# Moving weight blocks and activation blocks by lines of 64 bytes in a two-block transformer kernel, with matmuls in groups of two or four chunks

## What is computed

```python
# first stack, per layer
h = layer_norm(ALPHA * h + 0.5 * swiglu(h, ffn1...), ln1_g, ln1_b)
proj = h @ w_in                      # 20 column blocks of 128
mix = concatenate([ssd, fox, mla]) @ w_out
h = layer_norm(ALPHA * h + mix, ln2_g, ln2_b)
h = layer_norm(ALPHA * h + 0.5 * swiglu(h, ffn2...), ln3_g, ln3_b)
# second stack, per layer
x = x + 0.5 * swiglu_2(rmsnorm(x, ...), ffn1...)
x = x + mixers(rmsnorm(x, ...) @ w_in) @ w_out
x = x + 0.5 * swiglu_2(rmsnorm(x, ...), ffn2...)
```

## Time and profile before

| | us |
|---|---|
| median of three runs | 1946.86 (1946.73 to 1949.25) |
| profiled execution, its own time | 1947.75 |
| span of the profiled execution | 1945.9 |
| TensorE matmul busy | 1931.2 (99%) |
| TensorE weight load busy | 1892.7 (97%) |
| VectorE busy | 1431.5 (74%) |
| ScalarE busy | 1019.8 (52%) |
| GpSimd busy | 152.7 (8%) |

### The profile page before, as it was taken

One profiled execution on the slowest core, in us unless ns is written; L12 is line 12 of the kernel. 1 busy time (PEld: TensorE's weight loads), 2 busy tenths in 40 slices (PEclk: granted clock), 3 DMA queues, 4 the chain that ended last, 5 costly groups with the idle time before them and its releaser, 6 DMA issues.

```text
span 1945.9 us, 42335 instructions
## 1 busy us (share of the span) xinstructions
PE 1931.2 (99%) x16150; PEld 1892.7 (97%) x16150; DVE 1431.5 (74%) x2591; ACT 1019.8 (52%) x1527; POOL 152.7 (8%) x192
## 2 busy tenths in 40 slices
PE   9999999999999999999999999999999999999998
PEld 8999989999999999899999999999999999999998
DVE  6774787987588768879978874667765775667763
ACT  4443687554455447865547443665445444565443
POOL 0001123000100011320010100000000000100000
PEclk9999999999999999999999999999999999999999
DMA  7454433545454544345553665445555555435554
GB/s 265 172 197 170 166 109 112 192 174 193 156 192 172 196 164 145 109 152 194 201 191 140 235 233 183 151 149 185 193 214 177 195 202 208 152 131 195 194 213 154
DMA packets 46830, 346.66 MB, mean 178 GB/s; under 512 B 5344, under 2 KB 6416, under 8 KB 9232
## 3 DMA queue, kind: packets, MB, share of 16 engines
q1 hardware_dynamic: 44416, 335.63, 48.0%
q0 software_dynamic: 2320, 9.74, 1.6%
HBM read 344.29 MB, written 1.07 MB: 177 GB/s over the span
## 4 chain that ended last, share of the span: by engine, by line
PE 91%; DVE 4%; ACT 2%; DVEq 1%; issue 1%; DMA 0%; ACTq 0%; SPq 0%; POOL 0%
PE ps L622 22%; PE ps L623 22%; PE ps L624 22%; PE ps L639 14%; PE ps L630 2%; PE ps L631 2%; PE ps L632 2%; DVE w_lo L1996 1%; PE ps L1162 0%; DVE pj L2465 0%; DMA h<-in_hidden 0%; DVE cst L2486 0%; PE ps L1197 0%; DVE pj L2462 0%; ACT scratch L1669 0%
## 5 line engine op out<-in xcount | busy, mean ns | idle before, releaser
L1996 DVE TENSOR_TENSOR w_lo<-raw,w_hi 128x1024 fp32r<-128x1024 f32 (+1 forms) x582 | 749.3, 1313 | 151.1 <-ACT w_hi L1300 91.5
L622 PE MATMUL ps<-x_hi,w_lo 128*128 128x256 f32 (+3 forms) x2208 | 622.1, 282 | 1.5 <-DVE x_lo L2087 0.6
L624 PE MATMUL ps<-x_hi,w_hi 128*128 128x256 f32 (+3 forms) x2208 | 615.1, 279 | 0.0
L623 PE MATMUL ps<-x_lo,w_hi 128*128 128x256 f32 (+3 forms) x2208 | 614.8, 278 | 0.0
L1297 ACT ACTIVATE w_hi<-raw 128x1024 fp32r<-128x1024 f32 x454 | 466.3, 1052 | 92.5 <-PE ps L639 49.0
L622 PE MATMUL ps<-hid_hi,w_lo 128*128 128x256 f32 (+1 forms) x1536 | 431.5, 281 | 0.1
L624 PE MATMUL ps<-hid_hi,w_hi 128*128 128x256 f32 (+1 forms) x1536 | 430.2, 280 | 0.0
L623 PE MATMUL ps<-hid_lo,w_hi 128*128 128x256 f32 (+1 forms) x1536 | 429.8, 280 | 0.0
L622 PEld LDWEIGHTS ps<-x_hi,w_lo 128*128 128x128 f32 x2208 | 414.9, 188 | 6.4 <-issue 4.2
L623 PEld LDWEIGHTS ps<-x_lo,w_hi 128*128 128x128 f32 x2208 | 415.0, 188 | 0.5
L624 PEld LDWEIGHTS ps<-x_hi,w_hi 128*128 128x128 f32 x2208 | 414.6, 188 | 0.0
(11 more groups left out here) (351 smaller groups left out, 2315.3 us busy)
## 6 DMA issues: line engine op xcount, KB each, us to landing
raw<-in_w_up SPq DMA_DIRECT2D x176, 1024.0 KB, 4.8
raw<-in_w_down SPq DMA_DIRECT2D x64, 1408.0 KB, 6.0
raw<-in_w_in SPq DMA_DIRECT2D x36, 1024.0 KB, 4.8
raw<-in_w_out SPq DMA_DIRECT2D x16, 1024.0 KB, 4.8
cst<-row_copy POOLq DMA_DIRECT2D x2, 1088.0 KB, 8.5
raw<-in_w_up SPq DMA_DIRECT2D x4, 512.0 KB, 7.2
cst<-in_consts POOLq DMA_DIRECT2D x1, 1537.5 KB, 6.5
prm<-in_prm POOLq DMA_DIRECT2D x2, 690.0 KB, 7.2
```

Source lines behind the costliest of these rows:

```text
L622: mm(dst, low, xa, start=first, stop=False)
L623: mm(dst, high, xb, start=False, stop=False)
L624: return mm(dst, high, xa, start=False, stop=last)
L1996: v.tensor_tensor(dst, src, high.bitcast(F32), ALU.subtract).then_inc(lo_done, 1)
```

## The change

It moves operands and reorders matmuls. The arithmetic is the same, and so is the number of matmuls. Core of the diff:

```diff
-        PLAIN_LO = [KD * X_PITCH + n * LINE for n in (0, 0, 5, 6)]
-        PLAIN_AT, PLAIN_W = 640, max(PLAIN_LO) + KD * X_PITCH
+        PLAIN_AT, PLAIN_W = 640, 2 * KD * X_PITCH
...
-        x1_hi, x1_lo = chunks(x_hi_all[:, 2 * LINE:], KD, X_PITCH), chunks(x_lo_all, KD, X_PITCH)
+        x1_hi, x1_lo = chunks(x_hi_all, KD, T1), chunks(x_lo_all, KD, T1)
+        cat1_hi, cat1_lo = chunks(x_hi_all[:, 2 * LINE:], KD, X_PITCH), chunks(x_lo_all, KD, X_PITCH)
...
+        def plain_of(T):
+            pitch = T1 if T == T2 else X_PITCH
+            return chunks(plain, KD, pitch), chunks(plain[:, KD * pitch:], KD, pitch)
+
+        GROUP = {T1: 4, T1 + 2: 2, T2 + 2: 4}
         TIGHT = Place(P, 0, 0)
-        OPENING = Place(P, LINE, LINE)
-        BESIDE_274 = Place(P + 2 * LINE, 3 * LINE, LINE)
+        OPENING = Place(P + LINE, 0, 2 * LINE)
+        BESIDE_274 = Place(P + 2 * LINE, LINE, 3 * LINE)
         LEVEL_274 = Place(P + 2 * LINE, LINE, 3 * LINE)
-        BESIDE_258 = Place(P + 2 * LINE, LINE, 0)
+        BESIDE_258 = Place(P + LINE, 2 * LINE, 0)
+
+        ENTRY = {0: Place(P + 2 * LINE, 3 * LINE, LINE), 1: Place(P + 2 * LINE, 0, 2 * LINE)}
+
+        def entry_place(level):
+            return ENTRY.get(level, TIGHT)
...
-            def three_beside(dst, high, low, xa, xb, first, last):
...
-            def in_pairs(dst, high, low, xa, xb, T):
+            def in_groups(dst, high, low, xa, xb, T, size):
 
-                for k in range(0, KD, 2):
+                for k in range(0, KD, size):
                     for w, x in ((low, xa), (high, xb), (high, xa)):
-                        for c in (k, k + 1):
+                        for c in range(k, k + size):
                             last = mm(dst, w[:, c, :], x[:, c, 0:T], start=w is low and c == 0,
                                       stop=w is high and x is xa and c == KD - 1)
...
-                if T == T1 + 2 and place is not TIGHT:
-                    last = in_pairs(dst, high, low, xa, xb, T)
+                if T in GROUP and place is not TIGHT:
+                    last = in_groups(dst, high, low, xa, xb, T, GROUP[T])
...
-                N = T + 4 if T == T2 else T + 2
-                xs, place = (plain_hi, plain_lo_of(LEVEL_NORM[norm])), level_place(T)
+                N, xs, place = T + 2, plain_of(T), level_place(T)
...
-                unit(turn0, 1, 0, second_pieces)
-                unit(turn0, 1, 1)
+                entry = entry_place(LEVEL_NORM[norm])
+                unit(turn0, 1, 0, second_pieces, entry)
+                unit(turn0, 1, 1, {}, entry)
```

More of the change, by code:

```diff
@@ L304, in cat1 @@
         def cat1(T):
-            return x_of(T)
+            return (xt_hi, xt_lo) if T == T2 else (cat1_hi, cat1_lo)
         def hid_of(T):
@@ L624, in three @@
                 return mm(dst, high, xa, start=False, stop=last)
-            def three_beside(dst, high, low, xa, xb, first, last):
-                if first:
-                    mm(dst, high, xa, start=True, stop=False)
-                mm(dst[:, 0:T2 + 2], low, xa[:, 0:T2 + 2], start=False, stop=False)
-                step = mm(dst[:, 0:T2], high, xb[:, 0:T2], start=False, stop=False)
-                return step if first else mm(dst, high, xa, start=False, stop=last)
-            def in_pairs(dst, high, low, xa, xb, T):
-                for k in range(0, KD, 2):
+            def in_groups(dst, high, low, xa, xb, T, size):
+                for k in range(0, KD, size):
                     for w, x in ((low, xa), (high, xb), (high, xa)):
-                        for c in (k, k + 1):
+                        for c in range(k, k + size):
                             last = mm(dst, w[:, c, :], x[:, c, 0:T], start=w is low and c == 0,
@@ L667, in first_pair @@
                         high, low = (narrow_at(w, TIGHT, 0, u)[:, k, :] for w in (w_hi, w_lo))
-                        step = three_beside if T == T2 + 4 else three
-                        last = step(ps[:, bank + u, 0:T], high, low, xa[:, k, 0:T], xb[:, k, 0:T],
-                                    n == 0, n == KD - 1)
+                        last = three(ps[:, bank + u, 0:T], high, low, xa[:, k, 0:T], xb[:, k, 0:T],
+                                     n == 0, n == KD - 1)
                         if n == KD - 1:
@@ L1315, in hi_next, with second_pair @@
                 hi_unit(j, u, W_NARROW, place)
-            def second_pair(turn, u):
+            def second_pair(turn, u, place=TIGHT):
                 act.wait_ge(raw_landed[1], turn * 16 + 16)
                 act.wait_ge(unit_used, turn * 4 + (u - 1 + START))
-                hi_unit(1, u, W_NARROW)
+                hi_unit(1, u, W_NARROW, place)
             def load_log_exp():
@@ L2135, in level_down @@
                     if last and not crossing:
-                        lo_unit(turn0 + DOWN_T, 1, 0, W_NARROW)
+                        lo_unit(turn0 + DOWN_T, 1, 0, W_NARROW, entry_place(after[0] if after else None))
                     dve.drain()
@@ L2174, in level_up @@
                 ha, hb = hid_of(T)
-                def columns(block, n):
-                    if T == T2:
-                        v.tensor_reduce(wsum[:, 2 * n:2 * n + 2], block[:, T:T + 4].rearrange("p (h c) -> p c h", h=2), AX_X, ALU.add)
-                        dve.drain()
-                        return wsum[:, 2 * n + 1:2 * n + 2]
-                    v.tensor_copy(wcol[:, n:n + 1], block[:, T:T + 1])
-                    return block[:, T + 1:T + 2]
                 def pair(it, j, width):
@@ L2187, in pair @@
                     dve.wait_ge(unit_used, turn0 * 4 + it * 4 + (2 * j + 1 + START))
-                    v.scalar_tensor_tensor(out=silu[:, j, 0:T], in0=neg_mean[:, 0:T], scalar=columns(gate, 2 * j),
+                    v.tensor_copy(wcol[:, 2 * j:2 * j + 1], gate[:, T:T + 1])
+                    v.scalar_tensor_tensor(out=silu[:, j, 0:T], in0=neg_mean[:, 0:T], scalar=gate[:, T + 1:T + 2],
                                            in1=gate[:, 0:T], op0=ALU.mult, op1=ALU.add)
@@ L2196, in pair @@
                     dve.wait_ge(unit_used, turn0 * 4 + it * 4 + (2 * j + 2 + START))
[L2197 removed]
+                    v.tensor_copy(wcol[:, 2 * j + 1:2 * j + 2], upb[:, T:T + 1])
+                    v.scalar_tensor_tensor(out=half, in0=neg_mean[:, 0:T], scalar=upb[:, T + 1:T + 2],
                                            in1=upb[:, 0:T], op0=ALU.mult, op1=ALU.add).then_inc(up_free, 1)
```

37 lines of the change are left out of this document (15 added, 22 removed).

## The result

Seven executions of each kernel, taken in turn: 1953.6 us after (1953.4 to 1953.75), 1949.1 us before (1946.73 to 1949.6), ratio 1.0031 with a 95% interval of 1.0022 to 1.0040. Against the 1946.9 us from which the forecast was made it is 6.7 us more. The profiled execution after took 1953.73 us, its span 1951.9.

What follows compares the result with a forecast made beforehand. TensorE's matmul pace, start to start, was taken to bound the kernel, with no wait or transfer able to give much. Terms -3.6 - 2.0 - 0.3 = -5.9 us took 1946.9 to 1941.0 us, range 1936.0 to 1947.4.

Steps and rivals of the forecast that it cites:

- Opening: Opening loop, 960 matmuls of 272 columns: constant distance takes them from 123.7 to 120.0 ns each, 3.6 us less.
- the signs named in advance: Signs of a wrong forecast, among them opening loop at 123 ns or more, or widely spread durations in constant-distance loops.
- The other bound, 125.1: Opening loop: pace per matmul in ns if it took the uneven state's overhead, 113.3 + 11.8; 1.3 us more.
- 258 columns: Loop of the 256-token level stage, 960 matmuls: from 118.8 to 116.7 ns each, 2.0 us less.
- Level loops: 274-column loops, code inside unchanged: either may end up even or uneven; no net change, bounds 2.6 us either way.
- The two entered alike: The two 274-column level loops: claimed entered alike before the change, yet came out differently, at 123.3 and 126.0 ns.
- Second pairs -0.3, in-projections nothing: Second pairs of the 274-column level stages: 0.3 us less together; in-projections at distance 2 instead of 0: no change.
- The rule weighed against it: TensorE's two read ports are independent and never wait, so no distance in lines matters: sum 0.0 against -5.9 us.
- D: Rival: constant distance locks all these loops into the uneven state, 4.4 us slower, 1951.3 us; chance 0.08.
- C: Rival: distance in lines has no effect, overheads follow from columns and entry; 1946.9 us; chance 0.16.
- A: Rival: everything lands, and the second level loop and the in-projections turn even too; 1937.4 us; chance 0.20.
- B: Rival: one of the two new loops lands, the other stays or turns uneven; about 1944 us; chance 0.18.

Runs made afterwards that it cites:

- the one of 4530 us: One execution of the changed kernel with opening and 256-token level stage taken back, left out, cause unknown: 4530.2 us; the other ten had median 1949.1 us.

## Why the prediction was wrong, point by point

**What bounds the kernel**: right. TensorE's pace decided it all; no wait, queue or transfer took part, before or after.

**Opening, -3.6 forecast, +2.0 measured.** The step that failed is "I take 120.0, by the row that is nearest: 272 is, as 256, a whole number of lines, and both are continuous". None of some 140 stretches of 272 columns, over five combinations of pitches and three orders, came below 123.3 ns. 256 columns do not carry to 272: the good pattern of 256 takes 113.3, that of 272 takes 123.3, 10 ns more for 6.7 ns of columns, and as much as 274 columns in their even state. Nor was continuity what made 256 columns fast: at distance 0 they have it too and take 120.0 ns. The opening before, at 123.7, was within 0.4 ns of the best of all these stretches, so at most 0.4 us was to be won. Of the signs named in advance the loop at 123 or more came; the wide spread of durations did not (285 to 291 ns, before 284 to 291), though the step was wrong. The other bound, 125.1, was too low by 0.7 as well: uneven patterns cost different amounts in different layouts.

**258 columns, -2.0 forecast, +2.9 in the loop, +2.4 in the stage, +2.1 to 2.4 in the time.** The step that failed is "Nearest is the 274-column loop ... even state 107.5 + 9.2 = 116.7". An overhead was carried from one layout to another, and from distance 0 to 3. What the runs put in its place: 121.8 ns at distance 3, and 118.5 at 2, where the overhead is 11.0. At distance 2 the stage gains 0.7 us in the trace and some 0.5 by kind of execution, at distance 3 it loses 2.4.

**Level loops, no net change forecast.** The bounds were right, the middle was not. With the change's second pairs both loops were uneven in all three profiles, and every time but the one of 4530 us fits that; before, one of them was even in 31 of 74 executions. Against the executions from which I started this is the full 2.6 us. Of these the starting point is partly luck: from the upper kind of before, 1949.3, the same change costs 4.3 us. "The two entered alike" was the wrong reading here: their second pairs differ, and the slower kind went with the uneven loop each time.

**Second pairs -0.3, in-projections nothing**: the second pairs gave 0.1, the in-projections nothing, 1949.2 and 1949.1 in the two runs. The 0.3 was too much: from starts rounded to 0.1 us the slower second pair was read at 129 ns, where the trace has 127.8, and in pairs it runs at 126.0 and not at the even 123.3.

**VectorE, weight writes, DMA, nothing**: right.

**The rule weighed against it.** The Trainium skill, SBUF — State Buffer, "Who interferes with whom", gives TensorE independent ports for the two streams and lets it wait for nobody. With every other engine idle, 256 columns took 113.3 ns or 120.0 and 258 columns 118.4 or 121.7, by the addresses alone. The measurement decides: the sum by that rule, 0.0, was nearer to the truth than mine, for a reason that isn't its own. That the two read streams meet somewhere in the memory would fit this dependence on addresses, but no run shows that they do, or where.

**Rivals.** D had the right side, and both points from which it was to decide came true (first level loop at 126.0, opening above 124.5). Its mechanism did not hold as a rule: a locked distance is not in itself worse than a drifting one. Distance 2 at 258 columns is constant and the fastest, and so is distance 3 at 272 columns with 20 and 8 lines (123.3); the drifting layouts of 272 columns, chunk by chunk at 18 and 8 lines, lie at 124.5 to 126.0 for all but the opening's own. Its price was too small, since it took the uneven state of one layout for all: 1.3 + 0.5 where 2.0 + 2.4 were due. C fell with the runs of the opening alone and of the 256-token stage alone, A and B on the paces.

**What stays open.** Why the same program reaches the even state in one execution and not in another; why the opening's layout sat at 125.6 in the first stretch of one kernel and at 123.7 at its full addresses; why moves of it gave 125.6 in one list and 123.7 in the next; by what mechanism addresses set the pace at all.

## What to carry to other kernels

An overhead per matmul measured in one layout says little about another, even if both look regular: before operands are moved by lines, run the candidate order, pitches and distances as short stretches of TensorE alone, which here reproduced the kernel's loops to 0.2 ns where a layout had one pattern, and missed by 2.2 ns where it had two (the opening in pairs). Run each stretch several times, and the kernel too: where one layout has several stable patterns, a single profile or three timed runs can show a state that half the executions don't reach, and a change should then be compared by kind of execution. Take a mean over whole cycles of the pattern: cut elsewhere, one and the same cycle reads as 123.68 or 123.77 ns. Check what the best layout can give at all before costing a move to it.

## What the runs showed that I had not expected

- The pace of identical matmuls depends on the distance between the activations' and the weights' addresses modulo four lines of 64 bytes: 256 columns 113.3 to 120.0 ns, 258 in fours 118.4 to 121.7, with no other engine at work. Second stretches confirm the four values of 256 columns, the kernels those of 258 at distances 2 and 3; for 274 in pairs, 125.5 to 127.9, distances 1 to 3 stand on one stretch each. With repeats, moves of the opening's tensors by four or eight lines changed nothing.
- A loop can hold one of several patterns of gaps between starts for its whole length. At 274 columns in pairs, 18 and 10 lines, distance 0, these are 123, 123, 124 (123.3 ns) and 121, 123, 124, 125, 137 (126.0); at 272 columns in pairs the means are 123.3 and 125.6.
- With the second pairs of before, the pace of the 48 matmuls ahead of a level loop tells its state: 126.1 ns ahead of four even loops, 127.8 ahead of six uneven ones.
- 272 and 274 columns have the same best pace, 123.3 ns.
